# x and the first three weight chunks of a two-layer trunk kernel: loaded, split and multiplied in smaller parts, with fewer products of ones ahead

## The reference

```
x += 0.5 * SwiGLU(RMSNorm(x))                    first half-step FFN
x += W_o( sig(gA)*W_a(DSA) + sig(gB)*W_b(GLA) )  token mixers
x += 0.5 * SwiGLU(RMSNorm(x))                    second half-step FFN
x += sigmoid(RMSNorm(x) W_g) * (p[i] W_p)        per-layer input
```

```
def rmsnorm(x, g):
    y = xf * lax.rsqrt(jnp.mean(xf * xf, axis=-1, keepdims=True) + EPS)
    return (y * g.astype(jnp.float32)).astype(x.dtype)
```

## Time and profile before

| | us |
|---|---|
| median of three runs | 1176.69 |
| profiled execution | 1176.79 |
| its span in the trace | 1175.0 |
| PE busy | 1166.5 (99%) |
| DVE busy | 820.4 (70%) |
| ACT busy | 608.7 (52%) |
| POOL busy | 117.3 (10%) |
| first product of weights | 8.22 |
| last product | about 1169.4 |

### The profile page before, as it was taken

The page is one execution under the profiler, slowest core; times in us unless marked ns, Lnnn a source line. Parts: engine busy times, 40 slices in busy tenths (PEclk is TensorE's granted clock), DMA queues, the critical chain, the costliest instruction groups (busy, mean ns, idle before and its releaser), DMA issues.

```text
span 1175.0 us, 24023 instructions
## 1 busy us (share of the span) xinstructions
PE 1166.5 (99%) x10522; PEld 1142.7 (97%) x10522; DVE 820.4 (70%) x929; ACT 608.7 (52%) x685; POOL 117.3 (10%) x130
## 2 busy tenths in 40 slices
PE   9999999999999999999999999999999999999997
PEld 8999999999999999999999999999899999999997
DVE  6866545697978766655786665458799787666556
ACT  6544445555745644444764443447467556444454
POOL 2000001012512000001110000100134020000011
PEclk9999999999999999999999999999999999999999
DMA  7655554545445555555546555554544366556551
GB/s 292 233 202 190 192 203 176 186 151 203 150 145 197 201 190 204 187 192 198 185 181 218 185 208 182 189 212 140 216 145 150 139 216 211 193 187 208 180 180 37
DMA packets 33384, 218.87 MB, mean 186 GB/s; under 512 B 5184, under 2 KB 6016, under 8 KB 7296
## 3 DMA queue, kind: packets, MB, share of 16 engines
q1 hardware_dynamic: 33280, 217.34, 53.2%
HBM read 216.15 MB, written 1.05 MB: 185 GB/s over the span
## 4 chain that ended last, share of the span: by engine, by line
PE 98%; DVE 1%; DMA 1%; ACT 0%; SPq 0%; issue 0%; DVEq 0%
PE psum L399 32%; PE psum L400 31%; PE psum L401 31%; PE psum L681 1%; PE psum L660 1%; DMA x_all<-in_x 1%; PE psum L533 0%; PE psum L594 0%; PE psum L644 0%; PE psum L715 0%; PE psum L726 0%; PE psum L629 0%; PE psum L749 0%; DVE hB_lo L1720 0%; DVE gates L1752 0%; PE psum L576 0%
## 5 line engine op out<-in xcount | busy, mean ns | idle before, releaser
L1278 DVE TENSOR_TENSOR w_lo<-raw,w_hi 128x2048 fp32r<-128x2048 f32 x200 | 458.0, 2293 | 218.7 <-ACT w_hi L888 218.6
L888 ACT ACTIVATE w_hi<-raw 128x2048 fp32r<-128x2048 f32 x201 | 385.3, 1917 | 352.3 <-PE psum L401 344.4
L399 PE MATMUL psum<-hA_hi,w_hi 128*128 128x256 f32 x1360 | 377.6, 278 | 0.0
L400 PE MATMUL psum<-hA_hi,w_lo 128*128 128x256 f32 x1360 | 375.7, 276 | 0.0
L401 PE MATMUL psum<-hA_lo,w_hi 128*128 128x256 f32 x1360 | 375.6, 276 | 0.0
L399 PEld LDWEIGHTS psum<-hA_hi,w_hi 128*128 128x128 f32 x1360 | 255.3, 188 | 2.7 <-issue 2.7
L400 PEld LDWEIGHTS psum<-hA_hi,w_lo 128*128 128x128 f32 x1360 | 255.3, 188 | 0.0
L401 PEld LDWEIGHTS psum<-hA_lo,w_hi 128*128 128x128 f32 x1360 | 255.3, 188 | 0.0
L399 PE MATMUL psum<-hB_hi,w_hi 128*128 128x256 f32 x832 | 229.9, 276 | 1.3 <-DVE w_lo L1728 1.3
L400 PE MATMUL psum<-hB_hi,w_lo 128*128 128x256 f32 x832 | 229.7, 276 | 0.0
L401 PE MATMUL psum<-hB_lo,w_hi 128*128 128x256 f32 x832 | 229.7, 276 | 0.0
(11 more groups left out here) (204 smaller groups left out, 1239.7 us busy)
## 6 DMA issues: line engine op xcount, KB each, us to landing
raw<-in_weights SPq DMA_DIRECT2D x203, 1024.0 KB, 4.8
raw<-in_weights SPq DMA_DIRECT2D x2, 512.0 KB, 6.4
out<-gates SPq DMA_DIRECT2D x3, 256.0 KB, 2.3
x_all<-in_x SPq DMA_DIRECT2D x1, 520.0 KB, 3.6
x_all<-in_x SPq DMA_DIRECT2D x1, 512.0 KB, 6.4
relu<-in_p SPq DMA_DIRECT2D x2, 256.0 KB, 5.1
consts<-in_consts SPq DMA_DIRECT2D x1, 384.0 KB, 5.5
out<-gates SPq DMA_DIRECT2D x2, 128.0 KB, 2.3
```

The lines of the kernel that those rows point to most:

```text
L399: pe.matmul(o, lh, rh, start=start, stop=False)
L400: pe.matmul(o, ll, rh, start=False, stop=False)
L888: act.activation(w_hi[:, s, :], raw[:, s, :], ACT.Copy).then_inc(hi_ready[s], 1)
L1278: dve.tensor_tensor(w_lo[:, s, :], raw[:, s, :], w_hi[:, s, :].bitcast(F32), ALU.subtract).then_inc(lo_ready[s], 1)
```

## The change

The order at the start is cut finer. SP loads x in fourths, and after each fourth of x one fourth of chunk 0 and one of chunk 1; then chunk 2 in halves: 14 DMAs in place of 6, in the order x0, w0.0, w1.0, x1, w0.1, w1.1 and so on. ACT and DVE take them in that order, and ACT makes the squares of pairs 0, 1 and 2 right behind the fourths of the same number; the squares of pair 3 come after the halves of chunk 2. PE multiplies a fourth of chunk 0 and a fourth of chunk 1 in turn (`first_chunks`), and chunk 2 in two halves of four row blocks into banks 5 and 6 (`third_chunk`). The two products of the mean move from ahead of chunk 3 to the middle of its first column half. The products of ones ahead are 11 in place of 18. The other FFNs keep the old order (`chunks_in_pieces`).

```
-WARM = 18
+WARM = 11
 ...
+            for i in range(4):
+                part = slice(*X_FOURTHS[i])
+                sp.dma_start(x_all[:, part], a["x"][:, part]).then_inc(x_landed[i], 16)
+                for n in range(2):
+                    sp.dma_start(raw[:, n, piece(i)], a["weights"][n, :, piece(i)]).then_inc(piece_landed[n][i] if i < 3 else landed[n], 16)
             for i in range(2):
-                part = slice(*X_HALVES[i])
-                sp.dma_start(x_all[:, part], a["x"][:, part]).then_inc(x_landed[i], 16)
                 half = slice(1024 * i, 1024 * i + 1024)
-                sp.dma_start(raw[:, 0, half], a["weights"][0, :, half]).then_inc(landed[0] if i else half_landed, 16)
-            chunk(0, 1)
-            chunk(0, 2)
+                sp.dma_start(raw[:, 2, half], a["weights"][2, :, half]).then_inc(landed[2] if i else half_landed, 16)
...
+                    if q == 3 and L + f == 0:
+                        by_columns(s, b, h, (0,), range(4))
+                        mean_everywhere(L, k, 4)
+                        by_columns(s, b, h, (0,), range(4, 8))
...
+            def first_chunks(h):
+
+                for m in range(4):
+                    if m < 3:
+                        pe.wait_ge(piece_lo, m + 1)
+                    else:
+                        operands(0, 0)
+                    pe.wait_ge(h_ready, of_norm(0, 0, m + 1))
+                    for c in range(2):
+                        mm = pairs(0, 0, h, c, (2 * m, 2 * m + 1))
+                    if m == 3:
+                        mm.then_inc(chunk_done[0], 1)
+                    if m < 3:
+                        pe.wait_ge(next_lo, m + 1)
+                    else:
+                        operands(0, 1)
+                    for c in range(2):
+                        mm = pairs(1, 2, h, c, (2 * m, 2 * m + 1))
+                mm.then_inc(chunk_done[1], 1)
+
+            def third_chunk(h):
+
+                for i in range(2):
+                    if i:
+                        operands(0, 2)
+                    else:
+                        pe.wait_ge(half_lo, 1)
+                    for c in range(2):
+                        mm = pairs(2, THIRD_BANKS, h, c, range(4 * i, 4 * i + 4))
+                mm.then_inc(chunk_done[2], 1)
...
+            for m in range(4):
+                act.wait_ge(x_landed[m], 16)
+                for c in (2 * m, 2 * m + 1):
+                    ins = act.activation(hB[0][:, c, :], x[:, c, :], ACT.Copy, scale=first_gains[:, c:c + 1])
+                ins.then_inc(h_hi_ready, 1)
+                act.wait_ge(piece_landed[0][m] if m < 3 else landed[0], 16)
+                act.activation(w_hi[:, 0, piece(m)], raw[:, 0, piece(m)], ACT.Copy).then_inc(piece_hi if m < 3 else hi_ready[0], 1)
+                act.wait_ge(piece_landed[1][m] if m < 3 else landed[1], 16)
+                act.activation(w_hi[:, 1, piece(m)], raw[:, 1, piece(m)], ACT.Copy).then_inc(next_hi if m < 3 else hi_ready[1], 1)
+                if m < 3:
+                    squares(0, 0, m)
             for i in range(2):
...
+                half = slice(1024 * i, 1024 * i + 1024)
+                act.wait_ge(landed[2] if i else half_landed, 16)
+                act.activation(w_hi[:, 2, half], raw[:, 2, half], ACT.Copy).then_inc(hi_ready[2] if i else half_hi, 1)
             squares(0, 0, 3)
```

More of the change, by code:

```diff
@@ L32 @@
 UP_BANKS = (6, 7, 0, 1, 2, 3)
+THIRD_BANKS = 5
 SLOTS = 3
@@ L479, in ffn @@
                 mm.then_inc(chunk_done[s], 1)
[L480 to L494, removed]
@@ L1352, in ffn @@
                     chunk_products(L, n)
-                    dve.tensor_tensor(gate_sum, products(2 * g), both(rb), ALU.mult).then_inc(gate_scaled, 1)
+                    dve.tensor_tensor(gate_sum, high(THIRD_BANKS) if L + f == 0 and g == 1 else products(2 * g), both(rb), ALU.mult
+                                      ).then_inc(gate_scaled, 1)
                     if g:
@@ L1730, in _ @@
-            for i in range(4):
-                if i < 3:
-                    dve.wait_ge(next_hi, i + 1)
+            for m in range(4):
+                dve.wait_ge(x_landed[m], 16)
+                dve.wait_ge(h_hi_ready, of_norm(0, 0, m + 1))
+                for c in (2 * m, 2 * m + 1):
+                    ins = dve.scalar_tensor_tensor(out=hB[1][:, c, :], in0=x[:, c, :], scalar=first_gains[:, c:c + 1],
+                                                   in1=hB[0][:, c, :].bitcast(F32), op0=ALU.mult, op1=ALU.subtract)
+                ins.then_inc(h_ready, 1)
+                if m < 3:
+                    dve.wait_ge(piece_hi, m + 1)
+                else:
+                    dve.wait_ge(hi_ready[0], 1)
+                dve.tensor_tensor(w_lo[:, 0, piece(m)], raw[:, 0, piece(m)], w_hi[:, 0, piece(m)].bitcast(F32), ALU.subtract
+                                  ).then_inc(piece_lo if m < 3 else lo_ready[0], 1)
+                if m < 3:
+                    dve.wait_ge(next_hi, m + 1)
@@ L1733, in _ @@
                 else:
                     dve.wait_ge(hi_ready[1], 1)
-                next_piece(i)
-            split(0, 2)
+                next_piece(m)
+            for i in range(2):
+                half = slice(1024 * i, 1024 * i + 1024)
+                if i:
+                    dve.wait_ge(hi_ready[2], 1)
+                else:
+                    dve.wait_ge(half_hi, 1)
+                dve.tensor_tensor(w_lo[:, 2, half], raw[:, 2, half], w_hi[:, 2, half].bitcast(F32), ALU.subtract
+                                  ).then_inc(lo_ready[2] if i else half_lo, 1)
```

99 lines of the change are left out of this document (46 added, 53 removed).

## The result

The changed kernel takes 1178.53 us (median of 22 executions, all but one of them from 1177.73 to 1180.89), the kernel before 1176.68 (22 executions, 1176.51 to 1177.07). The ratio is 1.0017, 95% interval 1.0011 to 1.0022: slower by 1.85 us, which is less than the 2.35 us that the prediction took as the least that can be told from no change. The one took 1968.43 us at a mean granted clock of 0.556 and is left out of the ratio. The prediction was 1175.9 us with a range of 1174.3 to 1177.2: the sign and the range were wrong.

What follows compares the result with a forecast made beforehand. TensorE's own work was taken as the bound (98% of the chain), so only its late start pays. Chunk 5 at 35.8 instead of 36.57 gains 0.75 us: span 1174.25, execution 1176.04, median 1175.9 us; range 1174.3 to 1177.2.

Steps and rivals of the forecast that it cites:

- the row of landings: Start loads: x0 lands at 3.65, chunk 0's first fourth 4.4, chunk 1's 5.45, x1 6.75, then one each 0.65 us.
- the meter: Start of chunk 5 on TensorE, taken as measure of the gain: 35.8 instead of 36.57, 0.75 us earlier.
- I take the curve unchanged: Start loads: small pieces follow the earlier kernel's curve of bytes moved, 0.42 MB per us after 6 us.
- Rival B: Start loads: small pieces land late at the ramp; first product 8.18, chunk 5 0.9 us later, 1177.6 us; chance 0.17.
- The first product: TensorE's start: first real product at 6.15 instead of 8.22, 2.07 us earlier.
- Meetings of GpSimd and VectorE: Fourths at the start: adds and VectorE block each other, some 0.55 us each; chunk 0's last w_lo 15.4 instead of 13.9.
- rival A: Fourths at the start: GpSimd and VectorE hardly meet; chunk 3 issued at 14.0, gain 2.2 us, 1174.5 us; chance 0.25.
- The late reload: Slot 0's reload with chunk 3: issued at 15.5 instead of 12.06, cover gone, TensorE stands 1 us.
- The landing of 4.8 us: Chunk 3's load into slot 0: takes 4.8 us from issue, so it has landed at 20.3.
- Rival C: Chunk 3's load: landing takes 5.7 or 6.4 us instead of 4.8; 1176.7 to 1177.5 us; chance 0.08.
- sign that it is wrong altogether: TensorE after the start: products at half rate after a small gap, or a new wait for chunk 4 or 5.
- The eleven products of ones cost nothing: TensorE's warm-up: passes end by 5.5, 0.7 us gap before the first product, no clock loss charged.

Runs made afterwards that it cites:

- e1: Changed kernel with 18 products of ones ahead instead of 11: 1177.54 us, ratio 1.0009.
- e3: Changed kernel with GpSimd's four adds for pairs 1 and 2 of the first norm cut to one column: 1177.78 us, ratio 1.0007.
- e4: Changed kernel's order of work, with x and chunks 0 and 1 loaded in interleaved halves instead of fourths: 1180.10 us, ratio 1.0028.
- e5: Changed kernel again, unchanged, on the same chip as others of the set: 1178.33 us, ratio 1.0015.
- e8: Changed kernel with chunk 3 loaded into the free half of gates instead of slot 0, queued right behind chunk 2: 1176.44 us, ratio 1.0000.
- e9: Changed kernel with chunk 3 in its own place in gates and 18 products of ones instead of 11: 1176.78 us, ratio 1.0002.
- e13: Changed kernel again, unchanged, in turn on one chip with its version with 18 products of ones: 1178.14 us, ratio 1.0013.
- e14: Changed kernel with 18 products of ones instead of 11, repeated in turn with the unchanged copy: 1177.74 us, ratio 1.0009.
- e15: Changed kernel, chunk 3 in its own place, squares of pairs 1 and 2 behind chunk 2's halves, pair 3's behind chunk 3's split: 1179.83 us, ratio 1.0027.
- e11: Kernel before, with chunks 1 and 2 each loaded by two DMAs of 0.5 MB with 2 KB rows: 1177.04 us, ratio 1.0003.
- e2: Kernel before in its old order, with x and chunks 0 and 1 loaded in fourths, chunk 2 in halves (14 DMAs): 1178.33 us, ratio 1.0014.
- e16: Kernel before, with chunk 1 alone loaded as four DMAs of 0.25 MB: 1177.27 us, ratio 1.0006.
- e12: Kernel before, with the 64 KB identity in eight DMAs, two ahead of each half of x, four ahead of chunk 2: 1177.92 us, ratio 1.0011.
- e7: Kernel before with 14 DMAs cut across partitions (by 64, chunk 1 by 32), rows 4 to 8 KB long: 1184.31 us, ratio 1.0065.
- e10: Kernel before, with only chunk 3 loaded into its own place in gates, right behind chunk 2: 1176.73 us, ratio 1.0000.
- e6: Kernel before with 11 products of ones ahead instead of 18: 1177.51 us, ratio 1.0005.

## Why the prediction was wrong

The step that failed is the row of landings; the meter that the prediction chose was sound, and the runs make it sharper. In the ten profiles with the new order (the changed kernel and e1, e3, e4, e5, e8, e9, e13, e14, e15) the span is the start of chunk 5's `w_lo` plus 1140.84 to 1140.95 us. And where chunk 3 is reloaded into slot 0 and chunk 4 lands within 2.44 us of it (e1, e5, e13, e14), that start follows the one of chunk 3's `w_lo` by 11.23 to 11.26 us, against 11.19 plus 0.05 in the prediction:

| | chunk 3 issued | landed | `w_lo` 3 starts | `w_lo` 5 starts | span |
|---|---|---|---|---|---|
| before | 12.06 | 17.8 | 22.57 | 33.76 | 1175.0 |
| predicted | 15.5 | 20.3 | 22.3 | 33.5 | 1174.25 |
| e13 (unchanged copy) | 16.53 | 21.44 | 23.39 | 34.65 | 1175.5 |
| e1 (18 products) | 16.76 | 21.6 | 23.56 | 34.79 | 1175.7 |
| e14 (18 products) | 16.90 | 21.92 | 23.87 | 35.12 | 1176.0 |
| e5 (unchanged copy) | 17.05 | 22.10 | 24.05 | 35.31 | 1176.2 |
| after, first profile | 17.08 | 21.97 | 23.92 | 36.15 | 1177.1 |
| e8 (own place) | 8.20 | 19.67 | 21.63 | 33.64 | 1174.5 |

In e8 the distance is 12.01, since there the row of VectorE waits for the mean's two products on TensorE (26.25), and TensorE sets the pace. From chunk 3's `w_lo` to the end the four take 0.16 to 0.20 us more than forecast; nearly all of the miss is in what comes ahead of it.

**Landings: the step that failed.** "I take the curve unchanged" put x1 at 6.75 and the rest of the row behind it. x1 came at 8.49, 1.74 us later (8.45 in e5, 7.57 in e13). In e5 this carries through: x1 1.70 us late, chunk 3 issued 1.55 late, its `w_lo` 1.75 late with a landing of 5.05 us instead of 4.8, the span 1.95 us over the forecast. The median is over that profile by another 0.34 us; the executions differ and the longer ones weren't all seen in a profile. The first two pieces were right (x0 at 3.39, chunk 0's first fourth at 4.46), and the curve of bytes was even met up to 6 us (1.12 MB moved); two things in it were wrong. The pieces were not completed in step with the bytes: x0, both first fourths and x1 hold 1.06 MB together, 1.12 MB were moved by 6 us, and x1 was complete 2.5 us after that, so the DMA engines must have been at work on the pieces behind it too. And from 6 to 14 us the rate was 347 GB/s instead of 421, most of that from 6 to 10 us. The evidence that was taken for it, rows of 2 KB at 395 GB/s, was true and beside the point: e11 shows that 2 KB rows in DMAs of 0.5 MB cost next to nothing. What costs is the cut into many small DMAs from the head of the queue on: e2 with all else as before, 1.47 us at chunk 1 and 1.65 in the time; four of them behind large ones, 0.33 (e16); two DMAs of 0.5 MB, 0.04 (e11). Rival B had the direction and the size (it decides from 0.75 us), but put the delay at the first two pieces, where there was none: its first product would be at 8.18, and it was at 5.94. Why small DMAs at the head are slower than the sum of their issues is open; tiny ones (e12) are not. That it is the short rows of the very first loads, and not their number, isn't excluded: e7, which was to tell the two apart, met a larger cost. The new order adds a dip at 6 to 8 us (265 GB/s, 301 with halves in e4, 374 in the old order in e2), whose cause is open too. The rule of the Trainium skill that the prediction set beside B (DMA: Bandwidth & Descriptors, Measured) is in the direction that the runs show; in size it is not borne out here, as the queue with the quarter-megabyte DMAs still moved 347 GB/s from 6 to 14 us.

**The first product** at 6.15: 5.94 in the first profile and in e5, 6.41 in e13. Right.

**Meetings of GpSimd and VectorE**: right in mechanism and size. Three VectorE instructions were lengthened by 0.47 to 0.61 us (e3), 0.55 was the figure; chunk 0's last `w_lo` was to end 8.65 us after x1 had landed (15.4 after 6.75) and ended 8.48 after it (16.97 after 8.49). Taking the adds away brought back 0.75 us of 1.85. So rival A was wrong. What the prediction takes from the Trainium skill (SBUF — State Buffer, Who interferes with whom), that the two engines block each other, agrees with the three instructions of e3.

**The late reload**: right in mechanism (SP held, cover gone, a wait of TensorE ahead of chunk 3: 0.76 to 0.93 us, about 1 forecast), wrong in size: issued 1.0 to 1.6 us later than forecast. e8 removes it and brings back 1.9 us; e10 shows that the kernel before has nothing to gain there. The landing of 4.8 us, the shorter of the two later ones in the earlier trace rows, was 4.9 to 5.05 in the unchanged copies. Rival C, a landing of 5.7 or more, did not come up in them (5.35 in e3 is the nearest but one without the adds). Something akin did: chunk 4, queued right behind, was 2.4 us behind chunk 3 or (first profile) 3.6, and the latter put 1.0 us on top. The sum has no term for chunk 4's landing. The prediction's own sign that it is wrong altogether, a new wait ahead of chunk 4 or 5, came up there: 0.43 us ahead of chunk 5 at 38.50, and 0.47 in e3.

**"The eleven products of ones cost nothing ... so I charge no clock."** For TensorE's time up to chunk 3 that holds in the profiles of this kernel: after the first product the granted clock stays 1.00, and whatever TensorE loses there is swallowed by the wait at 26 us. That the passes end by 5.5 was wrong for the first profile, where they started 0.21 us apart to the last (at 5.82 us), right up to the first product. In another order it fails: the same 11 products in the old order left a gap of 1.93 us and cost 0.88 us of time (e6), where 1.14 us had cost nothing. That 18 products took 0.99 and 0.40 us off the changed kernel in two comparisons (e1, e14) and put 0.34 on it in e8's form (e9) is not explained: the profiles show no way from the products of ones to the issue of chunk 3, and the same kernel's profiles differ by 0.5 us in that issue alone (16.53 to 17.08). The mean granted clocks of the executions don't point to a fall of the clock in the slower ones: in e5 the five slowest of the eleven, 1178.61 to 1179.40 us, have 0.999, the two fastest 0.997.

**What the change earns without its cost.** With the reload out of the way (e8) it is level with the kernel before, 1176.44 against 1176.63 on that chip, and not 2 us better. TensorE starts chunk 2's last product at 24.77, the kernel before at 25.03. Of the 2.3 us at the first product 2.0 are gone in waits between the fourths, where TensorE is through sooner than the next pieces land and are split.

## What to carry to other kernels

In this kernel a finer cut at the start bought the first product early and paid with the later landings. Before making such a cut, follow the buffer that must be loaded again: find when its last reader ends in the new order, and check whether the DMA engines stand idle between the last queued load and that reload (here 16 to 18 us, share 0.05). If they do, give the next chunk a place of its own, before anything is gained at the front; here that brought the time back to what it had been, and no further (e8). Whether it would have been enough to put all of chunk 0 ahead of chunk 1 in the order wasn't tried.

## What the runs showed of the hardware

- The time of the engines and the bytes part: at a DMA share of 0.99 to 1.05 the rate from 6 to 14 us was 421 GB/s with the six DMAs of before, 408 with eight (e11), 383 with the 14 of e2, and 347 and 367 with the 14 in the changed order (first profile, e5). In the changed kernel the difference is gone from 12 us on (411, and 413 before). At 64 and 32 partitions it was 237 (e7).
- Issues get dearer behind a full queue: 0.42 us each at first, up to 1.1 us for one in the changed kernel near 5 us (two issues at 4.00 take 1.68 us together):

```profile
4.00 1.68 SPq L380 DMA_DIRECT2D raw<-in_weights  x2
```
- TensorE's granted clock fell to 0.50 for some 3 us, starting about 1 us after the products had begun again, when 1.9 us without products followed 22 passes that had run 0.21 us apart, all but the last two of e4 (e4, e6). It stayed at 1.00 after gaps of 1.14 and even 2.63 us (e7) behind 36 passes, some twenty of them 0.11 us apart, and of 1.40 us in the changed kernel's stretch of products. So the length of the gap alone doesn't decide it.
- An add of GpSimd that meets the 2.29 us `w_lo` of a whole chunk takes up to 2.32 us instead of 0.74 (e15); one that meets the short instructions of the fourths takes 1.16 at most (changed kernel). The three VectorE instructions of e3 lost 0.47 to 0.61 us to a meeting, while that `w_lo` kept its 2.29.
